# The first layer's start: input tiles ahead of the weights, small constants, and the first query projection cut into tiles around the modulation products

## What is computed

```
m = (jax.nn.silu(cvec) @ w_mod + b_mod)[..., None, :]
shift, scale, gate = jnp.split(m, 3, axis=-1)
h = layer_norm(x) * (1 + scale) + shift
br = split_projection(h @ lw['w_in'])
qa = rms_norm(br['qa'], lw['q_norm'])          # then rotary positions on latent tokens
...
```

## Time and profile before

| | |
|---|---|
| median of 3 runs | 1411.04 us (1409.86 to 1411.09) |
| span of the profiled execution, first to last instruction | 1406.3 us |
| its device time | not listed apart from the three runs; the span leaves 4.7 us to their median |
| PE busy | 1353.3 us, 96% of the span |
| mean granted TensorE clock | 0.997 |
| instructions | 22404 |

### The profile page before, as it was taken

How to read it: one execution, slowest core, us unless ns; L and a number is a source line. 1 busy time by engine, 2 the same in 40 slices (tenths; PEclk the granted TensorE clock), 3 DMA queues, 4 the chain that set the end, 5 groups by cost and what they waited for, 6 DMA issues and landing times.

```text
span 1406.3 us, 22404 instructions
## 1 busy us (share of the span) xinstructions
PE 1353.3 (96%) x8624; PEld 1252.1 (89%) x8624; DVE 769.7 (55%) x1605; ACT 623.7 (44%) x1298; POOL 693.0 (49%) x500
## 2 busy tenths in 40 slices
PE   6998999999999999999999999999999999999997
PEld 4898989899888999999877988998989989999985
DVE  5756773263873511656694577722458715036557
ACT  4436876234764211213254478852367733222230
POOL 3455565334665354344663566642256554445453
PEclk9999999999999999999999999999999999999999
DMA  9312001122012244354321210012111042225321
GB/s 374 125 61 80 16 31 46 61 88 67 31 46 98 98 165 151 104 210 136 120 101 39 91 61 31 31 46 79 61 61 45 31 135 67 70 76 195 131 79 76
DMA packets 36762, 126.94 MB, mean 90 GB/s; under 512 B 5040, under 2 KB 5680, under 8 KB 36656
## 3 DMA queue, kind: packets, MB, share of 16 engines
q1 hardware_dynamic: 29952, 108.54, 22.5%
q10 hardware_dynamic: 6704, 16.97, 3.3%
HBM read 119.73 MB, written 5.77 MB: 89 GB/s over the span
## 4 chain that ended last, share of the span: by engine, by line
PE 86%; DVE 6%; POOL 3%; ACT 2%; issue 2%; DVEq 0%; POOLq 0%; ACTq 0%
PE ps L939 50%; PE ps L887 6%; PE ps L889 6%; PE ps L888 6%; PE ps L1082 4%; PE ps L1072 3%; PE ps L1074 2%; PE ps L1093 2%; PE ps L1094 2%; DVE x L1745 1%; PE ps L956 1%; POOL with_eps L1764 1%; POOL w_lo L1780 1%; POOL p_f_a L1806 1%; POOL rstd L1765 1%
## 5 line engine op out<-in xcount | busy, mean ns | idle before, releaser
L1780 POOL TENSOR_TENSOR w_lo<-raw,w_hi 128x1024 fp32r<-128x1024 f32 x148 | 361.9, 2452 | 265.3 <-ACT w_hi L1137 182.4
L939 PE MATMUL ps<-h_hi,w_hi 128*128 128x320 f32 x1280 | 295.7, 312 | 8.7 <-DVE g_c L1685 4.6
L939 PE MATMUL ps<-h_hi,w_lo 128*128 128x320 f32 x1280 | 292.0, 309 | 0.0
L939 PE MATMUL ps<-h_lo,w_hi 128*128 128x320 f32 x1280 | 291.5, 309 | 0.0
L939 PEld LDWEIGHTS ps<-h_hi,w_hi 128*128 128x128 f32 x1280 | 218.0, 188 | 25.4 <-DVE g_c L1685 6.0
L1137 ACT ACTIVATE w_hi<-raw 128x1024 fp32r<-128x1024 f32 x148 | 154.1, 1055 | 145.1 <-DMA raw<-in_weights 67.3
L939 PEld LDWEIGHTS ps<-h_hi,w_lo 128*128 128x128 f32 x1280 | 215.1, 188 | 1.8
L939 PEld LDWEIGHTS ps<-h_lo,w_hi 128*128 128x128 f32 x1280 | 215.2, 188 | 1.6
L887 PE MATMUL ps<-w_hi,h_hi 128*128 128x512 f32 (+1 forms) x360 | 129.3, 359 | 2.1 <-POOL w_lo L1780 2.0
L889 PE MATMUL ps<-w_hi,h_lo 128*128 128x512 f32 (+1 forms) x360 | 127.6, 354 | 0.0
L888 PE MATMUL ps<-w_lo,h_hi 128*128 128x512 f32 (+1 forms) x360 | 127.5, 354 | 0.0
(11 more groups left out here) (182 smaller groups left out, 2615.5 us busy)
## 6 DMA issues: line engine op xcount, KB each, us to landing
raw<-in_weights SPq DMA_DIRECT2D x190, 512.0 KB, 3.3
raw_more<-in_weights SPq DMA_DIRECT2D x10, 512.0 KB, 10.5
x<-in_x_sample ACTq DMA_DIRECT2D x6, 512.0 KB, 9.8
x_mid<-x ACTq DMA_DIRECT2D x5, 512.0 KB, 2.6
x<-x_mid ACTq DMA_DIRECT2D x5, 512.0 KB, 6.0
y_sample<-x SPq DMA_DIRECT2D x3, 512.0 KB, 2.6
pack<-in_pack ACTq DMA_DIRECT2D x2, 528.0 KB, 6.2
x<-in_x_sample SPq DMA_DIRECT2D x2, 512.0 KB, 5.1
```

The source lines that it names most:

```text
L939: last = pe.matmul(ps[:, s + half, 0:HALF], w[:, u % RING, cols], acts[:, k, half * HALF:(half + 1) * HALF], start=k == 0 and part == 0, s ...
L1780: did(pool.tensor_tensor(w_lo[:, n % RING, :], raw_tile(r), w_hi[:, n % RING, :], ALU.subtract), w_ready)
```

## The change

Six edits, all about the beginning of layer 0:

1. SP's queue takes x tiles 1, 3 and 4 ahead of the weights; ACT's queue takes x tile 0 first, then the constants, the identity alone, and x tile 2.
2. The constants shrink from 304 to 50 columns: `pick` was two 128-column blocks and is two columns. The block of ones, which the `bc` events late in each layer multiply by, is now a tile `ones` that POOL fills at the start.
3. The three masks are loaded later, with the rotary tables.
4. These late loads (rotary tables, masks, `pack`) move from p = 1 to p = 3.
5. In the list, the first two `nx` and `ht` stand ahead of the first modulation products, and `ht 3` and `nx 4` behind the last of them.
6. The query units are walked by tiles (event `mp`, the last tile remains in `mm`): tile 0 of unit p, the modulation products of p+1, tile 1, the columns of p+1, then tiles 2, 3 and 4.

```diff
@@ first_stages
-    out.extend([nx0, ("mod", 0, 0, 0), ("mod", 0, 0, 1), nx1, ht0, ht1, nx2, nx3, ("mod", 0, other, 0), ht2,
-                ("mod", 0, other, 1), nx4, ht3])
+    def tile(p, t):
+        return ("mp", 0, "q_a", p, t)
+
+    out.extend([nx0, nx1, ht0, ht1, nx2, ("mod", 0, 0, 0), ("mod", 0, 0, 1), nx3, ht2, ("mod", 0, other, 0),
+                ("mod", 0, other, 1), ht3, nx4])
     cols(0)
     out.extend([("split", 0), ht4, ("h", 0, 0), ("h", 0, 1)])
-    mods(1)
     for p in range(KT_D // 2):
         if p:
             out.extend(("h", 0, j) for j in (2 * p, 2 * p + 1))
             out.append(("split", p))
-        if p == 1:
+        if p == KT_D // 2 - 1:
             out.append(("load", 0, "pack"))
+        out.append(tile(p, 0))
         if p + 1 < KT_D // 2:
-            if p:
-                mods(p + 1)
+            mods(p + 1)
+        out.append(tile(p, 1))
+        if p + 1 < KT_D // 2:
             cols(p + 1)
-        out.append(("mm", 0, "q_a", p))
+        out.extend([tile(p, 2), tile(p, 3), ("mm", 0, "q_a", p)])
...
@@ def unit_pass
-                    pe.wait_ge(w_ready, u + 1)
+                    if tiles[0] == 0:
+                        pe.wait_ge(w_ready, u + 1)
...
-                    for t in range(T):
+                    for t in tiles:
...
@@ SP
-                for t in (1, 3):
+                for t in (1, 3, 4):
                     sp.dma_start(x[:, t, :], x_source(t)).then_inc(x_in[t], 16)
@@ ACT
+                load(x_in[0], x[:, 0, :], x_source(0))
                 load(const_loaded, consts[:, :], a["consts"])
-                load(x_in[0], x[:, 0, :], x_source(0))
-                load(setup_loaded, setup[:, :, :].rearrange("p s n -> p (s n)"), a["setup"])
-                for t in (2, 4):
-                    load(x_in[t], x[:, t, :], x_source(t))
+                load(setup_loaded, setup[:, 0, :], a["setup"][:, 0:P])
+                load(x_in[2], x[:, 2, :], x_source(2))
...
                             load(rope_loaded, rope[:, :, :, :].rearrange("p t c d -> p (t c d)"), a["rope"])
+                            load(masks_loaded, setup[:, 1:4, :].rearrange("p s n -> p (s n)"), a["setup"][:, P:4 * P])
```

More of the change, by code:

```diff
@@ L377, in flat, with unit_tiles @@
             yield e
+def unit_tiles(e):
+    return range(T - 1, T) if e[1:3] == (0, "q_a") else range(T)
 def weight_units(order):
@@ L524, in bank_plan @@
             take(e[2], 2, until=e[2])
+        elif kind == "mp" and e[3] == 0:
+            stage = ("in", e[1], e[2], e[4])
+            take(stage, 1, until=stage)
         elif kind == "mm" and e[3] == 0:
-            for t in range(T):
+            for t in unit_tiles(e):
                 stage = ("out", e[1], 0, t) if e[2] == "out0" else ("in", e[1], e[2], t)
@@ L627 @@
 PACK_SIZE = _at
[L628 removed]
+CONST_SIZE = 2 + 2 * KT_D + DEPTH * 2 * KT_D
 def build(nc, a, outs):
@@ L654, in build @@
         ident = ident_r[:, :].bitcast(F32)
-        pick = consts[:, 0:2 * P].rearrange("p (s n) -> p s n", s=2)
+        pick = consts[:, 0:2]
+        ones = sb("ones", [P, P])
         rope = sb("rope", [P, LAT, 2, HD])
-        _c = 2 * P
+        _c = 2
         c_in = consts[:, _c:_c + 2 * KT_D].rearrange("p (s j) -> p s j", s=2)
@@ L905, in in_ring, with unit_pass @@
                     return w_hi[:, u % RING, :], w_lo[:, u % RING, :]
-                def unit_pass(e):
-                    _, l, name, n = e
+                def unit_pass(e, tiles, closes):
+                    l, name, n = e[1:4]
                     width = WIDTH[name]
                     nk = UNIT // width
-                    u = USERS[e]
-                    pe.wait_ge(w_ready, u + 1)
+                    u = USERS[("mm", l, name, n)]
+                    if tiles[0] == 0:
+                        pe.wait_ge(w_ready, u + 1)
                     acts = (m_hi, m_lo) if name == "out0" else (h_hi, h_lo)
@@ L922, in unit_pass @@
                             did(last, filled[PLACE[stage][0]])
-                    if not ends:
+                    if closes and not ends:
                         did(last, w_used)
@@ L963, in _ @@
                         for n in range(2):
-                            last = pe.matmul(ps[:, s, 2 * n:2 * n + 2], mod_row[:, buf, n * P:(n + 1) * P], pick[:, 1, 0:2],
+                            last = pe.matmul(ps[:, s, 2 * n:2 * n + 2], mod_row[:, buf, n * P:(n + 1) * P], pick,
                                              start=True, stop=True)
@@ L969, in _ @@
                         s = begin(e)
+                        pe.wait_ge(zeroed, 3)
                         pe.wait_ge(mod_summed, 2 * GATE_MODS.index(("mod", l, 8 + g)) + 2)
                         for v in range(2):
-                            last = pe.matmul(ps[:, s, v * COLS:(v + 1) * COLS], pick[:, 0, :], mod_row[:, v, :],
+                            last = pe.matmul(ps[:, s, v * COLS:(v + 1) * COLS], ones[:, :], mod_row[:, v, :],
                                              start=True, stop=True)
@@ L1018, in _ @@
                         did(last, filled[s])
+                    elif kind == "mp":
+                        unit_pass(e, range(e[4], e[4] + 1), False)
                     elif kind == "mm":
-                        unit_pass(e)
+                        unit_pass(e, unit_tiles(e), True)
                     elif kind == "cr":
@@ L1773, in _ @@
                 pool.wait_ge(zeroed, 2)
+                did(pool.memset(ones[:, :], 1.0), zeroed)
                 for e in ORDER:
```

7 lines of the change are left out of this document (4 added, 3 removed).

## The result

| | before | after |
|---|---|---|
| median device time | 1411.07 us (4 runs, 1409.86 to 1412.62) | 1423.47 us (4 runs, 1423.27 to 1423.69) |
| span of the profiled execution | 1406.3 us | 1421.5 us |
| start of the first gate product | 59.83 | 74.97 |

A forecast was written before the change was run, and what follows sets the result against it. PE, busy 96% of the span, was taken as the bound. Holes +8.2, start -2.6 and clock 1.2 gave +6.8 us; rounded down to +6.7 on the median 1411.0, this made 1417.7 us, range 1413.8 to 1420.5.

The forecast's parts named there:

- clock term: In the products and first tiles, one clock fall after the first holes: 1.2 us, between 0 and 1.7.
- The later holes of 2.15 us stand alone between 9 us of work: Waits before units 1 to 3: no clock fall expected, as behind the earlier 2.01 us hole; priced at nothing.
- the clock falls at the later holes too: Rival at the waits before units 1 to 3: 1.7 us lost each, giving 1420 to 1423; chance 0.08.
- put the difference on the median: Final sum: the predicted delay was added to the median 1411.0, the 1406.3 execution's own device time being unlisted.
- The start: Edits 1, 2, 5: tile 4's transposes start at 17.7 against 20.38; gain 2.6 us, bounds 1.8 and 3.4.
- the product starts when its unit lands: Last product of b = 4: starts once its weight unit lands at 15.1, with ACT's copy at about 15.8.
- The holes: PE idles 3.6 and 0.9 us around the first tile and 2.15 us before each of units 1 to 3.
- The chain of 6.25 us: From the end of two columns through ACT and POOL to the next unit's weights: 6.25 us, unchanged by the edit.
- The second hole of 0.9: First tile: after three matmuls PE idles 0.9 us until the second h_lo at 24.0.
- The late loads: Tables and masks loaded later: DVE's work ends with POOL's last subtraction or 0.5 us behind; costed at nothing.
- The rest: Ones tile and bc products cost nothing; later work passes the delay through. Rival, partly taken up: +2 to +4, chance 0.10.
- The sum without the clock: From tile 4's transposes to the first gate: +8.2 from holes, -2.6 from the start, together +5.6; gate at 65.4.

The follow-up runs named there:

- the filled kernels: Changed kernel with filler matmuls in the three later weight waits, 1419.16 us; the same plus 32 idle matmuls before the first tile, 1417.35 us.
- whole units: Changed kernel with edit 6 undone, so the units are walked whole again and edits 1 to 5 stay: 1409.93 us.
- x tile 2 first: Changed kernel with edit 6 undone and x tile 2 moved ahead of the constants and identity on ACT's queue: 1412.32 us.
- x tile 2 on SP: Changed kernel with edit 6 undone and x tile 2 moved from ACT's queue to SP's, between tiles 3 and 4: 1409.40 us.
- all holes filled: Changed kernel with 20 filler matmuls before each of the three later weight waits and 32 idle ones before the first tile: 1417.35 us.
- tiles only: Kernel before the change with edit 6 alone added: 1425.86 us.
- products first: Changed kernel with the four modulation products of p = 1 put ahead of the first query tile: 1419.39 us.
- whole units, hole filled: Changed kernel with edit 6 undone and 16 idle matmuls in PE's hole before the columns of p = 1: 1408.35 us.
- the long filling: Changed kernel with 20 filler matmuls before each of the three later weight waits and 56 idle ones before the first tile: 1419.43 us.

## Why the prediction was wrong

Its direction and the place of each hole were right, its size was half of what came. The forecast without its clock term put the first gate at 65.4, and it came at 74.97, 9.6 us later. From start to start of the rows this divides as follows.

| stretch | predicted | measured | difference |
|---|---|---|---|
| end of tile 4's transposes | 18.8 | 19.60 + 1.06 = 20.66 | +1.9 |
| to the first tile | 3.6 | 3.7 | +0.1 |
| first tile to unit 1 | 2.3 + 1.86 + 1.37 + 0.86 + 4.1 + 2.15 = 12.6 | 14.6 | +2.0 |
| unit 1 to unit 2 | 11.7 | 13.7 | +2.0 |
| unit 2 to unit 3 | 11.7 | 13.7 | +2.0 |
| unit 3 to the gate | 6.86 | 8.54 | +1.7 |

- **The clock: this step failed.** "The later holes of 2.15 us stand alone between 9 us of work, like the 2.01 one: nothing for those." Each was followed by 3.4 us at 1.2 GHz with a shortfall of 1.7, and at the first hole 6.8 us at half clock cost 2.6 of work (3.4 less the 0.85 in which PE was idle). I took 1.2 for all of it; the filled kernels gave back 4.3 + 1.8 = 6.1 in the medians. The rival "the clock falls at the later holes too" had a chance of 0.08 and 1420 to 1423. The Trainium skill (TensorE: Matmul & The Clock Gate, "HAM oscillation — how this bites in real kernels") names a longest harmless gap. The holes of 2.0 us lie under it, and the trace does not bear it out: the clock fell behind them.
- **Why that step looked safe.** It rested on a single execution of the kernel before, whose 2.01 us hole has no fall behind it. The kernel with whole units has the same hole of 2.01 us, and a fall with a shortfall of 1.7; with x tile 2 first it is 3.4. What is behind such a hole differs from execution to execution.
- **The profiled execution was a good one.** I noted 4.7 us between its span and the median, and put the difference on the median, as if all of them were time outside the span. In all thirteen executions here that have both, the device time is 1.7 to 1.9 us above the span (1423.27 and 1421.5 for the kernel after). The profiled execution of before then took about 1408.1, 2.9 under its median. The 61 runs of the kernel before beside the experiments show what goes with this: six have a mean granted clock of 0.997, as the profiled one has, and spans of 1406.4 to 1406.8; eight have 0.993 and 1410.8 to 1411.3; the others, at 0.994 and 0.995, lie between. So the profiled execution is one of the few with the fewest falls; at which holes the others fell isn't recorded. It also accounts for spans that differ by 15.2 and medians by 12.4.
- **The start: mis-sized.** 2.6 us were predicted and 20.38 - 19.60 = 0.8 came in the trace (1.2 in the medians of whole units). The fourth unit did land at 15.1, as worked out, but its product started at 17.27 (the other half of b = 4 at 16.81), because in front of it PE had the transposes of tile 2, which waited until 15.77 for the normalized tile, and the other half. The step "the product starts when its unit lands" was wrong. The constants (25 KB) and the identity (64 KB) were not 0.8 us cheaper but the slowest transfers for their size, as the first group shows (issues of the kernel after: count, KB each, median us to landing), and x tile 2 behind them came later still, as DVE's rows show:

```profile
x<-in_x_prompt ACTq DMA_DIRECT2D x1, 512.0 KB, 5.1
x<-in_x_sample ACTq DMA_DIRECT2D x1, 512.0 KB, 9.4
setup<-in_setup ACTq DMA_DIRECT2D x1, 64.0 KB, 7.4
const_tile<-in_consts ACTq DMA_DIRECT2D x1, 25.0 KB, 6.4
```

```profile
9.03 0.23 DVE L1506 CAST ident_r<-setup 128x128 fp32r<-128x128 f32 x1 [0.29 <-DMA setup<-in_setup]
11.59 1.29 DVE L1411 BATCH_NORM_STATS2 bn<-x 128x6 f32<-128x512 f32 x2 [2.33 <-DMA x<-in_x_sample]
...
67.33 1.60 DVE L1519 CAST mask_r<-setup 128x384 fp32r<-128x384 f32 x1 [3.16 <-DMA pack<-in_pack]
...
71.29 3.39 DVE L1523 TENSOR_TENSOR table<-rope,pack 128x512 f32<-128x512 f32 x2
```

DVE waits 2.33 us for tile 2, its normalization is ready for PE at 15.77. Yet the kernel with x tile 2 on SP had this wait removed and won 0.5 us: PE's own order in front of the product (16 transposes, 16 products, 8 transposes, from 10.4 to 16.3) keeps it late. What stretches the 16 products to 1.94 us, where 8 take 0.64, stays open, but it does not decide: in the kernel with all holes filled the same 16 took 1.07, and PE then waited 1.40 us for the normalized tile 2 and went on at 15.84.
- **The holes: right, the work between them a little short.** First hole 3.71 (3.6 predicted). Later ones 2.00 to 2.02 in the rows, to which the modelled tail of the last matmul, 0.39 - 0.23 = 0.16, belongs: 2.15 from start to start. The chain of 6.25 us kept its length (6.20). The second hole of 0.9 lay under the slow clock; with the clock kept up it was 0.54. A round without a fall takes 49.61 - 37.45 = 12.2 us, as the kernel with all holes filled shows, and not 11.7: the six matmuls of a tile that stands by itself take 39.01 - 37.45 = 1.56, and I had 1.37, a fifth of a whole unit.

```profile
37.45 0.49 PE L902 MATMUL ps<-w_hi,h_hi 128*128 128x512 f32 x1
...
39.01 0.64 PE L981 MATMUL ps<-raw,silu_c 128*32 128x256 f32 x8
...
49.61 0.50 PE L902 MATMUL ps<-w_hi,h_hi 128*128 128x512 f32 x1
```

- **The late loads: right, with a smaller margin than thought.** DVE waited 3.16 us for `pack` at 67.33, the table work ended at 74.68, 1.2 us behind POOL's last subtraction (63.78 + 9.74 = 73.52) and not 0.5. PE waited for none of it.
- **The rest: right.** Nothing is taken up later: the first waits behind 75 us are those of before (0.36, 1.53 and 1.83 us, the latter two those of the earlier trace rows), and the spans differ by what the gates differ, 15.2 and 15.1.
- **The sum without the clock: too small, and near the medians by luck.** Holes and start give +5.6 by the prediction, and the median of the kernel with all holes filled is 6.3 over. But its first gate is at 68.76, 8.9 us behind that of before, and its span 9.2 us longer. Of the 3.3 us between 5.6 and 8.9, 1.9 is the start, and the rest mostly the longer rounds. The medians agree with the forecast only because that of before holds 2.9 us of falls that its profile doesn't show.

## What to carry to other kernels

A wait of 2 us on TensorE can cost its length and 1.5 us more in half-speed work behind it, so before splitting a long stretch of matmuls into pieces, ask whether each chain of the other engines still fits behind the piece that is left in front of its wait. That no fall follows one hole in one profile says nothing of the next; price each hole with and without its fall, and use the difference between span and device time of other runs to see whether the profiled execution is a typical one. Idle matmuls in an unavoidable hole are a cheap test of the clock's share, and sometimes a gain, if they are timed to end before the operands come.

## What the runs showed of the hardware

- The shortfall of the clock from 20 to 80 us was 1.7, 3.4, 5.1, 6.8 or 8.5 us in the profiles with any: single stretches had 1.7 or 3.4, and no other size was seen. In front of units 1 to 3 a fall began 0.2 to 1.4 us behind the end of a 2.0 us hole (at 39.7 for the one that ended at 38.98, at 52.3 in tiles only for the one that ended at 50.95).
- Whether a fall comes is not decided by the hole's length alone: of nine holes of 2.0 us in front of units 1 to 3, in the kernels after, tiles only and products first, two (38.81 and 36.96) were followed by none, and one came where the hole had been filled (26.2, whole units, hole filled).
- On ACT's queue 25 KB took 6.4 us from issue to landing and 64 KB 7.4, while the 512 KB of x tile 0 ahead of them took 5.1. Behind a second x tile they took 8.5 and 9.6.
- The filling matmuls cost the same at 128 columns (3.77 us for 32, 0.118 each) and at 192 (2.37 us for 20, 0.118 each). In the windows of the long filling, 21 to 25 us, the weight loads of PE are busy for 4.0 of 4 us beside it. That they set the pace is read from these two figures; no run tested it.
